# Order of products on TensorE in the feed-forward layers, and 64-blocks turned by a transpose on half of the partitions

## The chip, the core and the metric

The kernel runs on one core of a Trainium2 chip. It is written by hand for each engine: TensorE (PE, with its weight loads shown as PEld), VectorE (DVE), ScalarE (ACT), GpSimd (POOL), and SyncE (SP), which issues the DMAs. The metric is the device time of one execution in microseconds (us). Before the change the median of three runs is 1302.59 us (1301.69 to 1302.69).

## The reference

Everything is float32, with 256 tokens of 1024 channels. Three layers follow one another:

```
h = rwkv7_time_mix(x)                 # a recurrence over time, 16 heads of 64
x = layer_norm(ALPHA*x + h);  x = layer_norm(ALPHA*x + swiglu_ffn(x))      # ffn 0
h = moba_attention(x)                 # 16 heads of 64, causal
x = layer_norm(ALPHA*x + h);  x = layer_norm(ALPHA*x + swiglu_ffn(x))      # ffn 1
# second block: conv branch, sparse attention, cross attention, then
hf = rmsnorm(h) @ w_ff1;  h = h + square(relu(hf)) @ w_ff2                 # ffn 2
return rmsnorm(h)

def swiglu_ffn(x, w_in, w_down):      # w_in 1024 x 2*2816, w_down 2816 x 1024
    gate, up = split(x @ w_in, 2)
    return (silu(gate) * up) @ w_down
```

In ffn 2 the inner width is 4096 and there is one way in (`u`) instead of two (`g` and `u`).

## The kernel before

**Products in three parts.** A float32 operand of a large product is held as two fp32r tiles, high and low (`WH`, `WL` for weights, `AH`, `AL` or together `AHL` for activations, `HH`, `HL` for the inner activations of a feed-forward layer). `mm3` (L541 to L544) makes one product of three matmuls: high by high, high by low, low by high, all added up in one PSUM bank. A weight arrives as a piece of 1024 KB by DMA (`RG`); ACT rounds it to the high tile (L1506), DVE subtracts to get the low one (L2132). There are three such pairs of tiles, used in turn.

**The way in.** `wide_piece` computes 256 output channels for all 256 tokens from one piece, in two banks (m = 0, 1) and eight steps k of 128 input channels. A step (`wide_step`) is a pair of matmuls: a long one of 512 columns (L590; the high weight slice against `AH` and `AL` side by side, into the two halves of the bank) and a short one of 256 columns (L591; the low weight slice against `AH`, added to the second half). L590 and L591 run 864 times each, 54 pieces. The loops are m outside and k inside, but where the activations are just being made (`ready`: the first piece of ffn 0 and of ffn 1) k is outside. `wide_half` (L616, L618) does the same for 128 tokens at a time, with 256 and 128 columns, for two pieces. The last piece of each layer goes through `chan` (`mm3` with 256 columns).

**The way down.** `down(f, n, j, tt, ...)` adds the 256 inner channels of piece j to the output of 128 tokens (tt), for two output halves h of 512 channels in banks 4 + 2 tt + h. For each h and each of two slices m of inner channels, it runs `mm3`: stationary is a slice of `HH` or `HL`, moving are 512 columns of weights. That is 12 matmuls for a tt. The order is h outside, m inside. At the last j, the end of each h raises `s_dn` (for the last h of tt = 1, `s_wdone`). DVE waits for it in `ffn_parts` (L2274, then `ln_part` L2231 and L2234 for h = 0 and again for h = 1, `ln_scale`, and an L2132 for a later weight piece between the two tt) or, at the kernel's end, adds the sum to the residual (L2359).

**Turned blocks.** In the time mix, arrays hold two heads on partitions 0 to 63 and 64 to 127. `block_turn` (L929) and `turned` (L971) turn 64 x 64 blocks with an ordinary float32 matmul of the block against an identity; lower and upper partitions alternate. Together they turn 80 blocks on the lower partitions and 80 on the upper: 32 + 48 of each, over two halves of the heads. Elsewhere full 128 x 128 blocks are turned with `e.transpose` (L625, L673, L690, L755, L805, L1112).

The order of the work is the order of the code on each engine; semaphores tie the engines together. TensorE's program is one sequence. Of other engines only the lines that wait for it matter here.

Of the kernel before, what the change touches and what calls it, by code (L numbers as in the profile page):

```python
# [146 lines left out]
def build(nc, a, out):  # L147
    ctx = ExitStack()
    with ctx:
# [82 lines left out]
        ident = cst('ident')  # L232
# [169 lines left out]
        def half_k(k, tt):  # L402
            return slice(k * 256 + tt * 128, k * 256 + tt * 128 + 128)
# [136 lines left out]
        def mm3(e, o, l, r, start, stop):  # L540
            (lh, ll), (rh, rl) = l, r  # L541
            e.matmul(o, lh, rh, start=start, stop=False)  # L542
            e.matmul(o, lh, rl, start=False, stop=False)  # L543
            return e.matmul(o, ll, rh, start=False, stop=stop)  # L544
# [10 lines left out]
        def wsl(name, n, k, c0, c1):  # L555
            s = W[name] % NW
            return v3(WH[s], n)[:, k, c0:c1], v3(WL[s], n)[:, k, c0:c1]

        def tensor_program(e):
# [24 lines left out]
                        t = mm3(e, PS[b][:, m * 256:(m + 1) * 256], wsl(name, 256, k, m * 128, m * 128 + 128), act_k(k), k == 0, k == 7)  # L584
                t.then_inc(s_wdone, 1)

            def wide_step(name, b, m, k):

                wh, wl = wsl(name, 256, k, m * 128, m * 128 + 128)
                e.matmul(PS[b][:, :].rearrange("p (a t) -> p a t", a=2), wh, AHL[:, :, k * 256:k * 256 + 256], start=k == 0, stop=False)  # L590
                return e.matmul(PS[b][:, 256:512], wl, AH[:, k * 256:k * 256 + 256], start=False, stop=k == 7)  # L591

            def wide_piece(name, banks, ready=None):

                split_ready(name)
                if ready is None:
                    for m in range(2):
                        for k in range(8):
                            t = wide_step(name, banks[m], m, k)
                else:  # L600
                    for k in range(8):
                        if k % 2 == 0:
                            e.wait_ge(s_tl, ready + k // 2 + 1)
                        for m in range(2):
                            t = wide_step(name, banks[m], m, k)
                t.then_inc(s_wdone, 1)

            def wide_half(name, banks, tt, ready):

                if tt == 0:  # L610
                    split_ready(name)
                for k in range(8):
                    e.wait_ge(s_tl, ready + 8 * tt + k + 1)
                    for m, b in enumerate(banks):
                        wh, wl = wsl(name, 256, k, m * 128, m * 128 + 128)
                        e.matmul(PS[b][:, :].rearrange("p (a t) -> p a t", a=2)[:, :, tt * 128:tt * 128 + 128], wh, AHL[:, :, half_k(k, tt)],  # L616
                                 start=k == 0, stop=False)
                        t = e.matmul(PS[b][:, 256 + tt * 128:384 + tt * 128], wl, AH[:, half_k(k, tt)], start=False, stop=k == 7)  # L618
                if tt:
                    t.then_inc(s_wdone, 1)  # L620
# [96 lines left out]
            def down(f, n, j, tt, mem_units):  # L717

                if tt == 0:
                    split_ready(f'f{f}d{j}')  # L720
                    e.wait_ge(s_fhl, FFN_AT[f] + j + 1)
                    if j == 0:
                        e.wait_ge(s_mkvo, mem_units)
                for h in range(2):
                    for m in range(2):
                        c0 = m * 256 + tt * 128
                        hh = HH[:, j % 2, c0:c0 + 128], HL[:, j % 2, c0:c0 + 128]
                        t = mm3(e, PS[4 + 2 * tt + h][:, :], hh, wsl(f'f{f}d{j}', 1024, m, h * 512, h * 512 + 512),
                                j == 0 and m == 0, j == n - 1 and m == 1)
                    if (tt, h) == (1, 1):  # L730
                        t.then_inc(s_wdone, 1)
                    elif j == n - 1:
                        t.then_inc(s_dn, 1)

            def attention(A, i):
                at = A.at
# [187 lines left out]
            def block_turn(half, g, b):  # L924
                e.wait_ge(s_zb, 4 * half + g + 1)
                for n in range(4):
                    ns = slice(n * 64, n * 64 + 64)
                    for q in (slice(0, 64), slice(64, 128)):
                        t = e.matmul(PS[b][q, ns], Zq[q, g, ns], ident[q, q], start=True, stop=True)  # L929
                t.then_inc(s_zt, 1)  # L930

            decay(0)
# [31 lines left out]
            def turned(half, banks):  # L964

                for q in range(3):
                    for i, src in enumerate((BE, KA)):
                        b, o_ = (banks[i], 256 * q) if q < 2 else (banks[2], 256 * i)
                        for n in range(4):
                            for pp in E2:  # L970
                                t = e.matmul(PS[b][pp, o_ + 64 * n:o_ + 64 * n + 64], src[pp, 4 * half + n, 64 * q:64 * q + 64], ident[pp, pp],  # L971
                                             start=True, stop=True)
                        if q:
                            t.then_inc(s_tu, 1)

# [2032 lines left out]
```

## Time and profile before

| | |
|---|---|
| median of the runs | 1302.59 us |
| the profiled execution | 1302.25 us, its span 1300.4 us |
| PE busy | 1251.8 us, 96% |
| DVE busy, ACT busy | 901.3 us (69%), 641.2 us (49%) |
| L590 and L591 (way in), x864 each | 306.9 and 242.5 us busy |
| way down, x304 for each of L542, L543, L544 | 119.2, 118.6, 118.6 us busy |
| L929 and L971 (turned blocks), x128 and x192 | 4.1 and 6.0 us busy |

Busy times of matmuls overlap: a matmul is shown from its start to a modelled end, and the next one starts before that. What a matmul costs in a row of matmuls is the distance from its start to the next start, and the timeline gives that. A float32 product (not fp32r) stands in the trace as two records, which is why L971 has 192 records for 96 products. In the timeline a row with "x8" is eight equal instructions merged.

### The profile page before, as it was taken

Reading aid. Unit: us, or ns where it says so; the run is one execution under the profiler, and the core shown is the slowest. Engines: PE = TensorE matmul, PEld = TensorE weight load, DVE = VectorE, ACT = ScalarE, POOL = GpSimd, SP = SyncE. Lnnn points to the kernel's source line nnn. Section 1 sums busy time; section 2 is a strip of 40 time slices with the busy share of each in tenths; the row PEclk is TensorE's granted clock in tenths of the full one; section 3 lists DMA queues with packets and bytes.
Section 4 is the critical chain, followed back from the end, with each engine's and each line's share of the span. In section 5 each row is a group of like instructions: output and inputs, shape, how many; then the busy total and the mean of one; then the engine's idle time right before and its main releaser. Section 6 shows DMA issues by size and latency. Waiting matters only on the chain.

```text
span 1300.4 us, 22008 instructions
## 1 busy us (share of the span) xinstructions
PE 1251.8 (96%) x9332; PEld 1087.7 (84%) x9332; DVE 901.3 (69%) x1433; ACT 641.2 (49%) x966; POOL 69.7 (5%) x43
## 2 busy tenths in 40 slices
PE   6999998999999999999999998999999999999998
PEld 4788897888888988768888888999888987788886
DVE  7456766766655677656665567989999766665555
ACT  3433435464444455556444445444355556555553
POOL 0022000002000061000200010000000000000000
PEclk9999999999999999999999999999999999999999
DMA  9532201665555365326555537455544453355550
GB/s 306 171 109 88 75 4 58 204 227 194 195 195 181 110 229 180 114 94 226 195 194 184 186 117 241 134 162 169 163 150 158 141 162 104 123 201 191 192 179 33
DMA packets 156211, 205.97 MB, mean 158 GB/s; under 512 B 9904, under 2 KB 129840, under 8 KB 155984
## 3 DMA queue, kind: packets, MB, share of 16 engines
q1 hardware_dynamic: 156112, 204.55, 47.7%
q8 instruction: 74, 1.21, 0.4%
q14 instruction: 25, 0.20, 0.0%
HBM read 202.44 MB, written 1.05 MB: 156 GB/s over the span
## 4 chain that ended last, share of the span: by engine, by line
PE 72%; DVE 18%; ACT 7%; issue 2%; DMA 0%; DVEq 0%; SPq 0%; ACTq 0%
PE PS L590 15%; PE PS L542 11%; PE PS L544 11%; PE PS L543 11%; PE PS L591 8%; DVE WW L2132 5%; PE PS L949 4%; DVE PH L2717 4%; ACT WW L1506 2%; DVE PA L2371 1%; PE PS L880 1%; PE PS L920 1%; PE PS L1004 1%; ACT Xb L1535 1%; PE PS L656 1%
## 5 line engine op out<-in xcount | busy, mean ns | idle before, releaser
L2132 DVE TENSOR_TENSOR WW<-RG,WW 128x2048 fp32r<-128x2048 f32 x164 | 380.9, 2337 | 142.2 <-ACT WW L1506 142.0
L1506 ACT ACTIVATE WW<-RG 128x2048 fp32r<-128x2048 f32 x164 | 311.2, 1906 | 30.6 <-PE PS L544 25.4
L590 PE MATMUL PS<-AHL,WW 128*128 128x512 f32 x864 | 306.9, 399 | 0.5 <-DVE WW L2132 0.5
L591 PE MATMUL PS<-AHL,WW 128*128 128x256 f32 x864 | 242.5, 281 | 0.0
L542 PE MATMUL PS<-AHL,WW 128*128 128x256 f32 x704 | 203.4, 289 | 2.5 <-DVE AHL L2171 1.8
L543 PE MATMUL PS<-AHL,WW 128*128 128x256 f32 x704 | 199.2, 283 | 0.0
L544 PE MATMUL PS<-AHL,WW 128*128 128x256 f32 x704 | 199.2, 283 | 0.0
L590 PEld LDWEIGHTS PS<-AHL,WW 128*128 128x128 f32 x864 | 162.3, 188 | 41.0 <-DVE WW L2132 1.2
L591 PEld LDWEIGHTS PS<-AHL,WW 128*128 128x128 f32 x864 | 163.2, 189 | 1.2
L542 PEld LDWEIGHTS PS<-AHL,WW 128*128 128x128 f32 x704 | 134.9, 192 | 5.3 <-issue 3.7
L543 PEld LDWEIGHTS PS<-AHL,WW 128*128 128x128 f32 x704 | 135.0, 192 | 1.7 <-issue 1.4
L544 PEld LDWEIGHTS PS<-AHL,WW 128*128 128x128 f32 x704 | 134.9, 192 | 0.0
L542 PE MATMUL PS<-WW,HH 128*128 128x512 f32 x304 | 119.2, 392 | 0.4 <-issue 0.2
L543 PE MATMUL PS<-WW,HH 128*128 128x512 f32 x304 | 118.6, 390 | 0.0
L544 PE MATMUL PS<-WW,HL 128*128 128x512 f32 x304 | 118.6, 390 | 0.0
L1608 ACT ACTIVATE PF<-PS 128x256 f32<-128x256 f32 x110 | 36.2, 381 | 135.5 <-PE PS L591 135.3
L2717 DVE SCALAR_TENSOR_TENSOR PH<-PH,VB 128x256 f32<-128x256 f32 x240 | 97.8, 478 | 0.0
L2282 DVE TENSOR_TENSOR PF<-PF,PS 128x256 f32<-128x256 f32 x110 | 41.3, 417 | 51.9 <-ACT PF L1608 50.3
L542 PEld LDWEIGHTS PS<-WW,HH 128*128 128x128 f32 x304 | 57.1, 188 | 13.4 <-issue 1.1
L544 PEld LDWEIGHTS PS<-WW,HL 128*128 128x128 f32 x304 | 57.1, 188 | 12.6
L543 PEld LDWEIGHTS PS<-WW,HH 128*128 128x128 f32 x304 | 57.1, 188 | 10.8
L949 PE MATMUL PS<-PA,RG 128*128 128x256 f32 x256 | 58.4, 383 | 0.0
(369 smaller groups left out, 1848.3 us busy)
## 6 DMA issues: line engine op xcount, KB each, us to landing
RG<-in_ffn_w_in SPq DMA_DIRECT2D x44, 1024.0 KB, 5.2
RG<-in_w_ff SPq DMA_DIRECT2D x32, 1024.0 KB, 5.4
RG<-in_w_in SPq DMA_DIRECT2D x30, 1024.0 KB, 5.2
RG<-in_ffn_w_down SPq DMA_DIRECT2D x22, 1024.0 KB, 4.9
RG<-in_w_rkv SPq DMA_DIRECT2D x12, 1024.0 KB, 6.8
RG<-in_moba_w_qkv SPq DMA_DIRECT2D x12, 1024.0 KB, 7.4
RG<-in_w_o SPq DMA_DIRECT2D x4, 1024.0 KB, 7.7
RG<-in_wx_kv SPq DMA_DIRECT2D x4, 1024.0 KB, 5.6
```

Of the source, the lines that this page charges most:

```text
L542: e.matmul(o, lh, rh, start=start, stop=False)
L543: e.matmul(o, lh, rl, start=False, stop=False)
L544: return e.matmul(o, ll, rh, start=False, stop=stop)
L590: e.matmul(PS[b][:, :].rearrange("p (a t) -> p a t", a=2), wh, AHL[:, :, k * 256:k * 256 + 256], start=k == 0, stop=False)
L591: return e.matmul(PS[b][:, 256:512], wl, AH[:, k * 256:k * 256 + 256], start=False, stop=k == 7)
L656: t = e.matmul(MEM_AT[u], wv[:, k, u % 2 * 128:u % 2 * 128 + 128], MT[:, k, :], start=k == 0, stop=k == 7)
L949: t = e.matmul(PS[n][:, m * 256:m * 256 + 256], v3(ring(name), 256)[:, k, m * 128:m * 128 + 128], XM[slot][:, k, :], start=k == 0, stop=k ...
L1506: s.activation(WH[hi_n % NW], ring(SPLIT[hi_n]), ACT.Copy, bias=0.0, scale=1.0).then_inc(s_hi, 1)
L1608: t = s.activation(dst[:, 256 * m:256 * m + 256], PS[b][:, 256:512], ACT.Copy, bias=0.0, scale=1.0)
L2132: v.tensor_tensor(WL[lo_n % NW], ring(SPLIT[lo_n]), WH[lo_n % NW].bitcast(F32), ALU.subtract).then_inc(s_lo, 1)
L2282: t = v.tensor_tensor(dst[:, sl], dst[:, sl], PS[b][:, 0:256], ALU.add)
L2717: v.scalar_tensor_tensor(out=CV[:, k, :], in0=UB[:, k, i:i + 256], scalar=vec(f'cw{i}', k), in1=CV[:, k, :], op0=ALU.mult, op1=ALU.add).th ...
```

## The change

Three edits, all in TensorE's program. In the way in, eight long matmuls of a bank come first and then its eight short ones (with `ready`, four long and four short; in `wide_half` two long and two short). In the way down, both output halves take the products of one slice of `HH` (four matmuls), then of `HL` (two), before the next slice; both halves now end at the last two matmuls. In the turned blocks, the lower partitions use `e.transpose`, the upper ones keep the matmul.

```diff
-            def wide_step(name, b, m, k):
+            def wide_hi(name, b, m, k):
-                wh, wl = wsl(name, 256, k, m * 128, m * 128 + 128)
+                wh, _ = wsl(name, 256, k, m * 128, m * 128 + 128)
                 e.matmul(PS[b][:, :].rearrange("p (a t) -> p a t", a=2), wh, AHL[:, :, k * 256:k * 256 + 256], start=k == 0, stop=False)
+            def wide_lo(name, b, m, k):
+                _, wl = wsl(name, 256, k, m * 128, m * 128 + 128)
                 return e.matmul(PS[b][:, 256:512], wl, AH[:, k * 256:k * 256 + 256], start=False, stop=k == 7)
...
                     for m in range(2):
                         for k in range(8):
-                            t = wide_step(name, banks[m], m, k)
+                            wide_hi(name, banks[m], m, k)
+                        for k in range(8):
+                            t = wide_lo(name, banks[m], m, k)
                 else:
-                    for k in range(8):
-                        if k % 2 == 0:
-                            e.wait_ge(s_tl, ready + k // 2 + 1)
+                    for kp in range(4):
+                        e.wait_ge(s_tl, ready + kp + 1)
                         for m in range(2):
-                            t = wide_step(name, banks[m], m, k)
+                            for k in (2 * kp, 2 * kp + 1):
+                                wide_hi(name, banks[m], m, k)
+                        for m in range(2):
+                            for k in (2 * kp, 2 * kp + 1):
+                                t = wide_lo(name, banks[m], m, k)
...
-                for h in range(2):
-                    for m in range(2):
-                        c0 = m * 256 + tt * 128
-                        hh = HH[:, j % 2, c0:c0 + 128], HL[:, j % 2, c0:c0 + 128]
-                        t = mm3(e, PS[4 + 2 * tt + h][:, :], hh, wsl(f'f{f}d{j}', 1024, m, h * 512, h * 512 + 512),
-                                j == 0 and m == 0, j == n - 1 and m == 1)
-                    if (tt, h) == (1, 1):
-                        t.then_inc(s_wdone, 1)
-                    elif j == n - 1:
-                        t.then_inc(s_dn, 1)
+                o_ = [PS[4 + 2 * tt + h][:, :] for h in range(2)]
+                for m in range(2):
+                    c0 = m * 256 + tt * 128
+                    hh, hl = HH[:, j % 2, c0:c0 + 128], HL[:, j % 2, c0:c0 + 128]
+                    w = [wsl(f'f{f}d{j}', 1024, m, h * 512, h * 512 + 512) for h in range(2)]
+                    first, last = j == 0 and m == 0, j == n - 1 and m == 1
+                    for h in range(2):
+                        e.matmul(o_[h], hh, w[h][0], start=first, stop=False)
+                        e.matmul(o_[h], hh, w[h][1], start=False, stop=False)
+                    for h in range(2):
+                        t = e.matmul(o_[h], hl, w[h][0], start=False, stop=last)
+                        if last and (tt, h) != (1, 1):
+                            t.then_inc(s_dn, 1)
+                if tt:
+                    t.then_inc(s_wdone, 1)
...
-                    for q in (slice(0, 64), slice(64, 128)):
-                        t = e.matmul(PS[b][q, ns], Zq[q, g, ns], ident[q, q], start=True, stop=True)
+                    for q in E2:
+                        if q.start:
+                            t = e.matmul(PS[b][q, ns], Zq[q, g, ns], ident[q, q], start=True, stop=True)
+                        else:
+                            t = e.transpose(PS[b][q, ns], Zq[q, g, ns], ident[q, q])
```

`turned` gets the same edit as `block_turn`, and `wide_half` the same as the way in. No other engine's sequence changes.

On PE in ffn 0, the last steps of a way-in piece before (`PS3` is a bank, `WW` the weight tiles, `AHL` the activations):

```order
L590 MATMUL PS3<-AHL,WW 128x512
L591 MATMUL PS3<-AHL,WW 128x256
L590 MATMUL PS3<-AHL,WW 128x512
L591 MATMUL PS3<-AHL,WW 128x256
L590 MATMUL PS3<-AHL,WW 128x512
L591 MATMUL PS3<-AHL,WW 128x256
```

The same piece now, whole (L595 is the short matmul):

```order
L590 MATMUL PS2<-AHL,WW 128x512 [waits w_lo,ffn_summed]
L590 MATMUL PS2<-AHL,WW 128x512 x7
L595 MATMUL PS2<-AHL,WW 128x256 x8
L590 MATMUL PS3<-AHL,WW 128x512 x8
L595 MATMUL PS3<-AHL,WW 128x256 x8
```

Long and short no longer alternate: a bank takes eight of 512 columns, then eight of 256.

On PE, the first way down that follows, tokens tt = 0, before (`HH`, `HL` the inner activations; `PS4` is output half 0, `PS5` half 1):

```order
L542 MATMUL PS4<-WW,HH 128x512 [waits mem_out,ffn_lo,w_lo]
L543 MATMUL PS4<-WW,HH 128x512
L544 MATMUL PS4<-WW,HL 128x512
L542 MATMUL PS4<-WW,HH 128x512
L543 MATMUL PS4<-WW,HH 128x512
L544 MATMUL PS4<-WW,HL 128x512
L542 MATMUL PS5<-WW,HH 128x512
L543 MATMUL PS5<-WW,HH 128x512
L544 MATMUL PS5<-WW,HL 128x512
L542 MATMUL PS5<-WW,HH 128x512
L543 MATMUL PS5<-WW,HH 128x512
L544 MATMUL PS5<-WW,HL 128x512
```

The same twelve now (L742 and L743 take `HH`, L745 takes `HL`):

```order
L742 MATMUL PS4<-WW,HH 128x512 [waits mem_out,ffn_lo,w_lo]
L743 MATMUL PS4<-WW,HH 128x512
L742 MATMUL PS5<-WW,HH 128x512
L743 MATMUL PS5<-WW,HH 128x512
L745 MATMUL PS4<-WW,HL 128x512
L745 MATMUL PS5<-WW,HL 128x512
L742 MATMUL PS4<-WW,HH 128x512
L743 MATMUL PS4<-WW,HH 128x512
L742 MATMUL PS5<-WW,HH 128x512
L743 MATMUL PS5<-WW,HH 128x512
L745 MATMUL PS4<-WW,HL 128x512
L745 MATMUL PS5<-WW,HL 128x512
```

The count is the same. Half 0 (`PS4`) had its last matmul in the sixth place, and now has it in the eleventh; half 1 stays at the twelfth.

## Rows read from the trace of the kernel before

**Rows 1.** The page: busy time by engine, and granted TensorE clock by slice.
```profile
PE 1251.8 (96%) x9332; PEld 1087.7 (84%) x9332; DVE 901.3 (69%) x1433; ACT 641.2 (49%) x966; POOL 69.7 (5%) x43
...
PEclk9999999999999999999999999999999999999999
```
**Rows 2.** Waits of PE, longest in total: us, times, longest.
```profile
PE PS L820 <- DVE PA L2371: 7.5, 2, 7.2
```
**Rows 3.** Timeline of PE in ffn 1, way in: start, duration, instruction.
```profile
600.17 0.28 PE L591 MATMUL PS<-AHL,WW 128*128 128x256 f32 x1
600.29 0.40 PE L590 MATMUL PS<-AHL,WW 128*128 128x512 f32 x1
...
604.41 0.28 PE L591 MATMUL PS<-AHL,WW 128*128 128x256 f32 x1
```
**Rows 4.** Timeline of PE, 512 columns after a run of 256.
```profile
435.29 0.40 PE L542 MATMUL PS<-WW,HH 128*128 128x512 f32 x1
...
437.13 0.39 PE L544 MATMUL PS<-WW,HL 128*128 128x512 f32 x1
```
**Rows 5.** Timeline of PE, 256 columns after a run of 512.
```profile
423.77 0.28 PE L542 MATMUL PS<-AHL,WW 128*128 128x256 f32 x1
...
425.08 0.28 PE L544 MATMUL PS<-AHL,WW 128*128 128x256 f32 x1
```
**Rows 6.** Timeline of PE, two pairs of `wide_half` shown.
```profile
1110.72 0.34 PE L616 MATMUL PS<-AHL,WW 128*128 128x256 f32 x1
...
1112.58 0.33 PE L616 MATMUL PS<-AHL,WW 128*128 128x256 f32 x1
```
**Rows 7.** Timeline of PE, end of ffn 1.
```profile
765.39 0.39 PE L544 MATMUL PS<-WW,HL 128*128 128x512 f32 x1
...
766.52 0.39 PE L543 MATMUL PS<-WW,HH 128*128 128x512 f32 x1
```
**Rows 8.** Timeline of DVE after ffn 1, and PE's next wait, in brackets.
```profile
765.88 0.69 DVE L2231 SCALAR_TENSOR_TENSOR Sb<-Hb,PS 128x512 f32<-128x512 f32 x1 [2.03 <-PE PS L544]
...
769.59 2.29 DVE L2132 TENSOR_TENSOR WW<-RG,WW 128x2048 fp32r<-128x2048 f32 x1
771.79 0.68 DVE L2231 SCALAR_TENSOR_TENSOR Sb<-Hb,PS 128x512 f32<-128x512 f32 x1
...
780.94 1.09 PE L690 MATMUL PS<-CB,Sb 128*128 128x128 f32 x8 [1.46 <-DVE Sb L2205]
```
**Rows 9.** Timeline of ACT and PE after ffn 0.
```profile
449.38 0.81 ACT L1600 ACTIVATE Sb<-Sb,ST 128x512 f32<-128x512 f32 x1 [0.42 <-DVE ST L2244]
450.52 1.04 PE L690 MATMUL PS<-CB,Sb 128*128 128x128 f32 x8
```
**Rows 10.** Timeline of PE and DVE at the kernel's end.
```profile
1292.35 0.39 PE L544 MATMUL PS<-WW,HL 128*128 128x512 f32 x1
1292.77 0.69 DVE L2359 TENSOR_TENSOR Hb<-Hb,PS 128x512 f32<-128x512 f32 x1 [0.30 <-PE PS L544]
...
1293.70 0.39 PE L544 MATMUL PS<-WW,HL 128*128 128x512 f32 x1
...
1294.13 0.69 DVE L2359 TENSOR_TENSOR Hb<-Hb,PS 128x512 f32<-128x512 f32 x1 [0.67 <-PE PS L544]
```
**Rows 11.** Timeline of PE: turned blocks of the first half, and full transposes.
```profile
144.63 2.99 PE L971 MATMUL PS<-CB,PA 64*64 64x64 f32 x96
...
446.20 1.03 PE L690 MATMUL PS<-CB,Sb 128*128 128x128 f32 x8
```
**Rows 12.** Waits of ACT, 130 to 200 us: us, times, longest.
```profile
ACT KX L1762 <- PE PS L971: 15.2, 2, 8.9
```
**Rows 13.** Timeline of PE: from a full array to 64 rows of it.
```profile
488.38 0.28 PE L544 MATMUL PS<-AHL,WW 128*128 128x256 f32 x1
488.59 0.93 PE L782 MATMUL PS<-PH 64*128 64x128 f32 x8
```

More of the change, by code:

```diff
@@ L614, in wide_half @@
                     for m, b in enumerate(banks):
-                        wh, wl = wsl(name, 256, k, m * 128, m * 128 + 128)
+                        wh, _ = wsl(name, 256, k, m * 128, m * 128 + 128)
                         e.matmul(PS[b][:, :].rearrange("p (a t) -> p a t", a=2)[:, :, tt * 128:tt * 128 + 128], wh, AHL[:, :, half_k(k, tt)],
                                  start=k == 0, stop=False)
+                    for m, b in enumerate(banks):
+                        _, wl = wsl(name, 256, k, m * 128, m * 128 + 128)
                         t = e.matmul(PS[b][:, 256 + tt * 128:384 + tt * 128], wl, AH[:, half_k(k, tt)], start=False, stop=k == 7)
@@ L970, in turned @@
                             for pp in E2:
-                                t = e.matmul(PS[b][pp, o_ + 64 * n:o_ + 64 * n + 64], src[pp, 4 * half + n, 64 * q:64 * q + 64], ident[pp, pp],
-                                             start=True, stop=True)
+                                to, of = PS[b][pp, o_ + 64 * n:o_ + 64 * n + 64], src[pp, 4 * half + n, 64 * q:64 * q + 64]
+                                if pp.start:
+                                    t = e.matmul(to, of, ident[pp, pp], start=True, stop=True)
+                                else:
+                                    t = e.transpose(to, of, ident[pp, pp])
                         if q:
```

## The prediction, made before the changed kernel was run

> **What bounds the kernel now.** I read the page first: PE is busy for 96% of the span, the granted clock is at nine tenths or more of full in every slice (the 2.4 GHz level), and DVE, the next, has 69% [rows 1]. Then the waits of PE: the longest in total is 7.5 us, and it lies in the first stage [rows 2]. So in the feed-forward layers the time is the number of matmuls times their distance in a row, and other engines matter only where a layer ends. The distances come from the timeline, start to start, since the busy times of matmuls overlap.
>
> **The way in, 104 blocks.** Today long and short alternate. Twelve pairs take from 600.17 to 604.41, so a pair is 4.24 / 12 = 0.3533 us and eight pairs are 2.827 [rows 3]. No place of the trace has eight long ones and then eight short ones of this kind, but both changes of length occur between longer runs. After a run of 256 columns the first eight distances at 512 columns go from 435.29 to 437.13, 1.84 us, that is 0.230 each [rows 4]. Once settled they are closer: the five from 765.39 to 766.52 give 1.13 / 5 = 0.226 [rows 7]. After a run of 512 columns the first eleven distances at 256 columns take from 423.77 to 425.08, 1.31 us, so eight take 0.95 [rows 5]. A block of eight and eight then is 1.84 + 0.95 = 2.79, against 2.827: 0.037 less. What costs today is thus the change of length itself, not the length. 52 pieces have two such blocks each (54, less the two that use `ready`): 104 x 0.037 = 3.8 us. In the 30 pieces that follow a way down, the first eight long ones find PE settled at 0.226 to 0.227 and take 1.81 instead of 1.84: 30 x 0.03 = 0.9. Today's first pair there gains little from this, and I take off 0.3. Sum: **4.4 us less**. All of it lies on PE's own row with nothing beside it that would end later, since PE hardly waits for weights here.
>
> The bounds. If a long one against `AHL` costs what it costs today because it reads two stretches of memory, and not because of its neighbours, nothing is won: 0. At best each pair falls to 0.2265 + 0.12 = 0.3465 at once: 832 x 0.0068 = 5.7 us less. I take 4.4, since the evidence of rows 4 and 5 is on plain matmuls of the same lengths and type.
>
> **`ready` and `wide_half`.** With `ready` the blocks are four and four; the next piece then waits for its low weights, so nothing counts: 0. In `wide_half` eight pairs of 256 and 128 columns take from 1110.72 to 1112.58, 0.2325 a pair or 0.116 a matmul [rows 6], although 128 columns are half the work of 256. So each matmul, however short, seems to wait for its own weight load, and two long and two short ones have four loads as before: 0. If the short ones did cost half of 0.12 when side by side, two pairs would fall from 0.465 to 0.36, and 32 such groups would give 3.4 us; that is the bound below, and 0.3 us more is the bound above (32 x 0.01, if all four come to 0.12).
>
> The Trainium skill ("TensorE: Matmul & The Clock Gate", LDWEIGHTS) has a load take its columns divided by 1.2 GHz, whatever the product's length, which is an estimate of 107 ns for 128 columns; the 116 ns of rows 6 fit that, and the rule speaks for no gain in `wide_half`.
>
> **The way down, inside.** 912 matmuls before, 912 now, all of 512 columns, each with its own load. Neighbours of one length settle at 0.226 to 0.227 whichever bank or slice they use [rows 7], so the sharing of a slice is worth 0; nothing in the trace shows a second use of a slice to be cheaper. Bounds: a hundredth of a slot either way, 0.002 us, which is what these rows leave open by their rounding, 2 us in all.
>
> **The way down, at its end.** Here the change costs. Half 0 now ends with the eleventh matmul instead of the sixth, five slots later: from 765.39 to 766.52, 1.13 us [rows 7].
> - *ffn 1.* DVE starts on half 0 of tt = 0 at 765.88, 0.49 after the start of that matmul, having idled 2.03 us for it. From there it works without a gap worth naming: both halves, the scale, the low weights at 769.59 for 2.29 us, and at 771.79 half 0 of tt = 1, when its matmuls have been done for a while. So the later start of tt = 0 moves the whole chain by 1.13, and PE, which waits 1.46 us for the end of it already, waits 1.13 more [rows 8].
> - *ffn 0.* The same chain and the same 1.13. It ends with L1600, 449.38 + 0.81 = 450.19, and PE takes its transposes at 450.52 without having waited, so 0.33 us of cover less some 0.06 for the signal: 1.13 - 0.27 = 0.86 [rows 9].
> - *The end of the kernel.* Half 0 of tt = 1 is added at 1292.77, 0.42 after its L544 at 1292.35; half 1 at 1294.13, 0.43 after 1293.70. Now half 0 ends one slot before half 1, at 1293.47, so its add runs from 1293.90 for 0.69 us and half 1's starts at about 1294.62: 0.49 us later, and the norm, the scale and the output behind it too [rows 10]. Half 0 of tt = 0 also comes later, but has 3 us of slack.
>
> Sum: 1.13 + 0.86 + 0.49 = **2.5 us more**. Bounds: 1.6 (if ffn 0 had full cover) and 3.4 (three times 1.13).
>
> **The turned blocks.** 96 records of L971, two for each of 24 blocks below and 24 above, take 2.99 us from 144.63: 0.03 a record, and 0.12 for a lower and an upper block together, since records of different partitions run beside each other and records of the same ones follow at 0.06. A transpose stands in the trace with one record (eight for the eight of L690 [rows 11]), so a lower block has one instead of two. The upper block keeps its two, 0.12 in a row, and sets the pace: 0. Bounds below: if records went one by one at 0.03, 80 x 0.03 = 2.4 us less. Bounds above: if the transpose can't run beside the upper block's records, 80 x 0.06 = 4.8 us more; if PE has to be switched between transpose and product, as it does between a full array and 64 rows of it, where 0.21 us lie between two starts instead of the 0.12 of rows 5 [rows 13], it is 160 x 0.09 = 14.4 us more. ACT waits for `turned` [rows 12], so neither gain nor loss would be hidden for the first half of the heads. I take 0, as all turned blocks keep 64 x 64 tiles and no switch is in the code.
>
> The Trainium skill speaks against this edit: "TensorEngine Tiling (Array Packing)", Restrictions and Gotchas, has column tiling exclude the transpose mode for FP32 and FP32R input, and Key Properties has a change of tiling mode drain TensorE. By that, either the transposes run as ordinary products (0) or each is a switch, which is the 14.4 us case. The trace has no transpose on a 64 x 64 tile, so only the price of a switch is borne out, by rows 13.
>
> **Sum.** -4.4 + 2.5 + 0 = -1.9 us. The profiled execution took 1302.25 us, 1.85 more than its span, and 0.34 less than the median 1302.59; so 1300.35 for it, and 1300.7 us for the median.
>
> **Rivals.**
> - *A, the forecast*, 1300.7 us: chance 0.48. Its spread is 1299.3 to 1302.3 (way in between 3.2 and 5.7, ends between 1.6 and 3.4).
> - *B, alternation was not the cost*: the two stretches of `AHL` are, so way in 0, ends +2.5: 1305.1 us. For it: today's 0.3533 is only seen with `AHL` in two stretches. Against: rows 4 shows plain matmuls at 0.230 for a while after a change of length. Chance 0.13.
> - *C, cheaper than that*: the way in at its best (5.7) with `wide_half` or the turned blocks giving 2 us or more, or the ends hidden: about 1298 us. Against: PE's wait of 1.46 in rows 8, and rows 6. Chance 0.20.
> - *D, the transposes hurt*: from the point on at which a lower transpose can't share the array with the upper product. 1300.7 + 4.8 = 1305.5, or with a switch each way 1315.1. For it: no 64 x 64 transpose has been seen, and the upper partitions were left as they are. Against: nothing in the code changes the tile. Chance 0.12 and 0.07.
>
> 0.2%, 2.6 us, is about what can be told from no change. Faster by more (below 1300.0): C and a quarter of A, 0.32. Slower by more (above 1305.2): D and some of B, 0.22. Within: 0.46. The range takes in A, B, most of C and the cheaper D: 1298.0 to 1305.5 us, and leaves out the switch.
>
> **What would show it.** Way in: distances near 0.230 after the first long one, falling, and 0.12 for the short ones, eight and eight in 2.79. Wrong if the long ones stay at 0.236. Ends: PE's wait before the second L690 group after ffn 1 grows to 2.6 us, one of about 0.9 appears after ffn 0, and the second add at the end starts 0.9 to 1.0 us after the last matmul instead of 0.43. Turned blocks: the 48 blocks of `turned` for one half of the heads in 2.9 us again; 4.4 or more would be D. The forecast as a whole is wrong if the way in saves less than 3 us, or if the DVE chain at a layer's end turns out to start at another signal than half 0's.

## The result, and the profile after

The changed kernel takes 1339.28 us (median of 4 runs, 1337.85 to 1339.44), the kernel before 1302.14 us beside it (1300.98 to 1302.69). The ratio is 1.0284, 95% interval 1.0266 to 1.0302: slower by 37 us, where 1.9 us less was forecast, and above the forecast's range, which ended at 1305.5 us.

The page shows the same picture as before in its first line and another one in its last, and that is the first thing to read here (busy time by engine; granted clock by slice of 33.4 us):

```profile
PE 1289.1 (96%) x9252; PEld 1114.9 (83%) x9252; DVE 900.6 (67%) x1433; ACT 641.4 (48%) x966; POOL 69.8 (5%) x43
...
PEclk9999796999999999999999999999999999999999
```

PE has 80 records fewer and is busy for 37.3 us more; DVE and ACT do the same work in the same time. The clock, at 9 (90% or more) in every slice before [rows 1], is at 7 and 6 in the fifth and seventh slice. Both are in the time mix, where the turned blocks are. Stretch by stretch (busy time and count of each engine, granted clock, DMA share, GB/s):

```profile
130.00:140.00 10.00, 10.00 (x57) 5.07 (x57) 7.96 (x15) 2.56 (x5) 1.27 (x1) 0.94 0.71 249
140.00:150.00 10.00, 10.00 (x122) 8.84 (x123) 4.26 (x8) 0.77 (x2) 0.00 (x0) 0.72 0.01 2
...
160.00:170.00 10.00, 10.00 (x114) 7.88 (x116) 1.72 (x5) 3.69 (x11) 0.00 (x0) 0.52 0.00 0
...
210.00:220.00 10.00, 10.00 (x50) 6.38 (x48) 2.56 (x4) 1.65 (x4) 0.00 (x0) 0.53 0.01 2
220.00:230.00 10.00, 10.00 (x59) 6.56 (x59) 0.00 (x0) 1.57 (x5) 0.00 (x0) 0.50 0.00 1
```

For comparison a stretch of the kernel before with `turned` in it:

```profile
140.00:150.00 10.00, 9.85 (x271) 9.67 (x269) 6.86 (x13) 3.42 (x10) 0.00 (x0) 1.00 0.01 2
```

From 210 to 230 us PE is busy all the time by the profile, starts 109 records in 20 us (271 stood in the 10 us above, before), and runs at half of full clock (0.50 to 0.53, the 1.2 GHz level). DVE and ACT nearly stand still. The timeline of PE shows what it does (start, duration, instruction). L948 is the transpose of a lower block and L946 the product of an upper one, two records:

```profile
135.02 0.24 PE L948 MATMUL PS<-CB,Sb 64*64 64x64 f32 x1
135.19 0.33 PE L946 MATMUL PS<-CB,Sb 64*64 64x64 f32 x2
135.45 0.24 PE L948 MATMUL PS<-CB,Sb 64*64 64x64 f32 x1
...
141.44 0.31 PE L948 MATMUL PS<-CB,Sb 64*64 64x64 f32 x1
141.68 0.47 PE L946 MATMUL PS<-CB,Sb 64*64 64x64 f32 x2
142.08 0.31 PE L948 MATMUL PS<-CB,Sb 64*64 64x64 f32 x1
...
142.97 0.47 PE L896 MATMUL PS<-PA 64*64 64x128 f32 x1
```

A lower and an upper block together take 0.43 us at full clock (135.02 to 135.45), and 0.64 at half clock (141.44 to 142.08). Before they took 0.12 [rows 11]. Of the 0.43, 0.17 lie between the transpose and the product, and 0.26 from the product's first record to the next transpose. The 128 records of L896 that follow are slower too: from 142.97 to the start of L883 at 151.30 are 8.33 us, where the same work took 6.99 us before (136.74 to 143.73).

`turned` has the same pattern. The timeline further on, where L883 begins, `turned` begins (L994) and ends (L1011) in the first half of the heads, and where it and the `block_turn` behind it begin and end in the second:

```profile
151.30 1.14 PE L883 MATMUL PS<-CB,PA 64*64 64x2 f32 x32
152.38 0.24 PE L994 MATMUL PS<-CB,PA 64*64 64x64 f32 x1
...
165.62 0.36 PE L1011 MATMUL PS<-Sb,PA 64*64 64x64 f32 x1
...
206.19 0.24 PE L994 MATMUL PS<-CB,PA 64*64 64x64 f32 x1
...
219.44 0.31 PE L948 MATMUL PS<-CB,Sb 64*64 64x64 f32 x1
...
229.28 0.36 PE L1011 MATMUL PS<-Sb,PA 64*64 64x64 f32 x1
```

Each group of turned blocks is counted from its first start to the first start of what follows it. The four groups take 7.95 (135.02 to 142.97), 13.24, 13.25 and 9.84 us, 44.3 together. Before they took 1.92, 2.83, 2.80 and 1.87, 9.4 together: 34.9 us more. ACT pays in waiting. Over both halves of the heads (130 to 240 us) it waits 25.0 and 9.0 us for `turned`, where before, in the same two places, it waited 15.2 [rows 12] and 0.6:

```profile
ACT KX L1784 <- PE PS L992: 25.0, 2, 14.6
...
ACT KX L1787 <- PE PS L992: 9.0, 2, 4.5
```

The other two edits did what was forecast. In ffn 1, long (L590) and short (L595) matmuls in rows of eight:

```profile
636.64 2.00 PE L590 MATMUL PS<-AHL,WW 128*128 128x512 f32 x8
638.48 1.11 PE L595 MATMUL PS<-AHL,WW 128*128 128x256 f32 x8
639.43 1.78 PE L590 MATMUL PS<-AHL,WW 128*128 128x512 f32 x7
```

Eight and eight take 639.43 - 636.64 = 2.79 us, against 2.83 in [rows 3]. PE's waits for the two lines that make the input of its full transposes, at the ends of ffn 0 and ffn 1 among others (us in total, times, longest; before 2.0 in two for the first, and 1.8 in two, the longest 1.5, for the second):

```profile
PE PS L701 <- ACT Sb L1622: 2.7, 3, 1.0
PE PS L701 <- DVE Sb L2227: 2.6, 1, 2.6
```

The end of the kernel, PE's last two matmuls and DVE's last two adds, each pair in one row:

```profile
1330.37 0.61 PE L745 MATMUL PS<-WW,HL 128*128 128x512 f32 x2
```

```profile
1330.80 1.28 DVE L2381 TENSOR_TENSOR Hb<-Hb,PS 128x512 f32<-128x512 f32 x2 [1.05 <-PE PS L745]
```

The second add ends at 1332.08 and takes 0.69 [rows 10], so it starts at 1331.39, 0.79 after the last matmul at 1330.60.

### The profile page after: what moved, and what is told of

Same layout as the page of the kernel before. It is cut to its first block, busy times and chain, and to the rows that moved or that the text cites. A ratio compares the mean times of both kernels' runs of the same rounds, so it can differ in the third digit from the quotient of the medians.

```text
span 1337.6 us, 21848 instructions
## 1 busy us (share of the span) xinstructions
PE 1289.1 (96%) x9252; PEld 1114.9 (83%) x9252; DVE 900.6 (67%) x1433; ACT 641.4 (48%) x966; POOL 69.8 (5%) x43
## 4 chain that ended last, share of the span: by engine, by line
PE 73%; DVE 18%; ACT 7%; issue 2%; DMA 0%; DVEq 0%; SPq 0%; ACTq 0%
PE PS L590 14%; PE PS L595 7%; PE PS L542 6%; PE PS L544 6%; PE PS L543 6%; DVE WW L2154 5%; PE PS L742 5%; PE PS L743 5%; PE PS L745 5%; PE PS L968 4%; DVE PH L2739 4%; ACT WW L1528 2%; PE PS L992 1%; PE PS L896 1%; DVE PA L2393 1%
## 5 line engine op out<-in xcount | busy, mean ns | idle before, releaser
L590 PE MATMUL PS<-AHL,WW 128*128 128x512 f32 x864 | 216.9, 392 | 0.5 <-DVE WW L2154 0.5
L542 PE MATMUL PS<-AHL,WW 128*128 128x256 f32 x704 | 203.3, 289 | 2.1 <-DVE AHL L2193 1.3
L543 PE MATMUL PS<-AHL,WW 128*128 128x256 f32 x704 | 199.1, 283 | 0.0
L544 PE MATMUL PS<-AHL,WW 128*128 128x256 f32 x704 | 199.1, 283 | 0.0
L590 PEld LDWEIGHTS PS<-AHL,WW 128*128 128x128 f32 x864 | 157.0, 189 | 30.0 <-DVE WW L2154 0.9
L542 PEld LDWEIGHTS PS<-AHL,WW 128*128 128x128 f32 x704 | 134.9, 192 | 4.9 <-issue 3.3
L543 PEld LDWEIGHTS PS<-AHL,WW 128*128 128x128 f32 x704 | 135.0, 192 | 1.7 <-issue 1.4
L544 PEld LDWEIGHTS PS<-AHL,WW 128*128 128x128 f32 x704 | 134.9, 192 | 0.0
L595 PEld LDWEIGHTS PS<-AHL,WW 128*128 128x128 f32 x864 | 118.4, 190 | 8.8
L595 PE MATMUL PS<-AHL,WW 128*128 128x256 f32 x864 | 121.1, 282 | 0.0
L742 PE MATMUL PS<-WW,HH 128*128 128x512 f32 x304 | 118.7, 390 | 0.5 <-issue 0.3
L743 PE MATMUL PS<-WW,HH 128*128 128x512 f32 x304 | 118.8, 391 | 0.0
L745 PE MATMUL PS<-WW,HL 128*128 128x512 f32 x304 | 93.7, 389 | 0.0
L745 PEld LDWEIGHTS PS<-WW,HL 128*128 128x128 f32 x304 | 57.1, 188 | 12.1
L742 PEld LDWEIGHTS PS<-WW,HH 128*128 128x128 f32 x304 | 57.2, 188 | 11.8 <-issue 1.1
L743 PEld LDWEIGHTS PS<-WW,HH 128*128 128x128 f32 x304 | 57.2, 188 | 10.8
```

What stands on the lines that cost most here:

```text
L742: e.matmul(o_[h], hh, w[h][0], start=first, stop=False)
L743: e.matmul(o_[h], hh, w[h][1], start=False, stop=False)
L745: t = e.matmul(o_[h], hl, w[h][0], start=False, stop=last)
```

## The experiments

Ten kernels, each timed beside the kernel before on the same chip. Two theories on the transposes: **S**, that each change between a transpose and a product on TensorE empties it; **P**, that a 64 x 64 transpose is itself slow. A third question was whether the lower clock is a cause or a result.

| run | median us | before | ratio, 95% interval |
|---|---|---|---|
| e1_no_turn | 1300.44 | 1302.39 | 0.9982 [0.9973, 0.9991] |
| e2_turn_only | 1341.52 | 1302.39 | 1.0300 [1.0286, 1.0314] |
| e3_wide_only | 1298.51 | 1302.39 | 0.9970 [0.9959, 0.9981] |
| e4_down_only | 1304.81 | 1302.39 | 1.0022 [1.0012, 1.0032] |
| e5_group_control | 1302.78 | 1302.0 | 1.0006 [0.9997, 1.0015] |
| e6_turn_grouped | 1319.13 | 1302.0 | 1.0131 [1.0117, 1.0145] |
| e7_turn_far | 1309.86 | 1302.0 | 1.0058 [1.0043, 1.0073] |
| e8_early_end | 1297.7 | 1302.0 | 0.9966 [0.9954, 0.9979] |
| e9_wide16 | 1296.53 | 1302.2 | 0.9956 [0.9943, 0.9970] |
| e10_turn_first | 1309.61 | 1302.2 | 1.0058 [1.0045, 1.0072] |

### e1_no_turn: the change without the transposes

```diff
-                        if q.start:
-                            t = e.matmul(PS[b][q, ns], Zq[q, g, ns], ident[q, q], start=True, stop=True)
-                        else:
-                            t = e.transpose(PS[b][q, ns], Zq[q, g, ns], ident[q, q])
+                        t = e.matmul(PS[b][q, ns], Zq[q, g, ns], ident[q, q], start=True, stop=True)
```
The same in `turned`.

> The change without its transposes (way in and way down as changed, the turned blocks as before). Theory S (the transposes on 64 x 64 tiles cost nearly all of the 37 us, by lost overlap and by the clock that falls with it; the two other edits are worth what the prediction said): 1.9 us less than before, between 0.5 and 3.5 less; no half-clock stretch in the time mix. Rival R (the long-first order or the shared slice costs too, for example through the clock after the longer wait behind ffn 1): more than before by 3 us or more.

1.95 us faster than before: -1.9 was the forecast of the two edits it keeps. The changed kernel is 37.1 us slower than before, so 39.1 us of it go with the transposes.

### e2_turn_only: the kernel before with the transposes alone

The edit of e1, the other way round, on the kernel before.

> The kernel before with the transposes alone. Theory S: 1302 + 37 + 2 = 1341 us, within 2; a lower and an upper block together 0.43 us at the full clock and 0.64 at half, in place of 0.12, and the same half-clock stretches in the time mix. Rival R: under 1335, since a part of the loss belongs to the other edits.

39.1 us slower. The transposes are enough by themselves, and it is what e1 leaves for them: nothing hangs on the edits together.

### e3_wide_only: the way in alone

The first two hunks of the change, and `wide_half`.

> The kernel before with only the way in and wide_half reordered. The prediction's term: 4.4 us less (3.2 to 5.7). Rival W (the gain on the long and short matmuls of a row is given back at the ends of the pieces, where other engines set the time): under 1.5 us less. Eight long and eight short should take 2.79 us.

3.9 us faster, where 4.4 was the term. Summed over all 864 pairs, the distances from start to start fall from 306.5 us in the kernel before to 302.8, which is 3.7. In `wide_half` a group of four takes 460 ns against 464 before: 0, as forecast. Behind a way down the timeline of PE has the first eight long ones faster:

```profile
614.93 1.98 PE L590 MATMUL PS<-AHL,WW 128*128 128x512 f32 x8
616.74 1.11 PE L595 MATMUL PS<-AHL,WW 128*128 128x256 f32 x8
617.70 2.00 PE L590 MATMUL PS<-AHL,WW 128*128 128x512 f32 x8
619.54 1.12 PE L595 MATMUL PS<-AHL,WW 128*128 128x256 f32 x8
```

1.81 us for the eight at 614.93, and 1.84 for the next. A whole block behind a way down takes 2.77 us, but the first eight pairs behind a way down were faster before as well, 2.81 instead of 2.83. So each of the 104 blocks gains the same 0.037, 3.8 us in all, and the 0.6 that the forecast added for the 30 pieces behind a way down is not there.

### e4_down_only: the way down alone

The hunk of `down`.

> The kernel before with only the way down changed. The prediction's term: 2.5 us more (1.6 to 3.4), all at the ends of the three layers: 0.9 after ffn 0, 1.1 after ffn 1, 0.5 at the kernel's end. Rival C (the longer wait after ffn 1 also drops the granted clock, as one short half-clock stretch stands there in the changed kernel's trace and none in the one before): 3.5 us more or above, with a half-clock stretch behind that wait. Rival N (other work covers it): under 1 us more.

2.4 us slower, where 2.5 was the term. Its timeline of DVE after ffn 1, the first step on half 0 (idle before it in brackets):

```profile
768.49 0.69 DVE L2236 SCALAR_TENSOR_TENSOR Sb<-Hb,PS 128x512 f32<-128x512 f32 x1 [3.16 <-PE PS L734]
```

The timeline of PE there, the two groups of transposes:

```profile
783.53 1.09 PE L690 MATMUL PS<-CB,Sb 128*128 128x128 f32 x8 [2.58 <-DVE Sb L2210]
785.01 1.97 PE L690 MATMUL PS<-CB,Sb 128*128 128x128 f32 x8 [0.39 <-DVE Sb L2210]
```

DVE idles 3.16 us instead of 2.03, and PE 2.58 instead of 1.46 [rows 8]: 1.13 and 1.12 more, one for one, and what the forecast said. The second group takes 1.97 us, where it took 1.09 before. The granted clock is 0.66 over these 10 us, and was 1.00 there before:

```profile
783.00:793.00 10.00, 7.95 (x45) 7.35 (x46) 6.46 (x14) 7.06 (x15) 0.00 (x0) 0.66 0.91 296
```

### e5_group_control: four lower blocks, then four upper, all as products

```diff
-                for n in range(4):
...
-                    for q in (slice(0, 64), slice(64, 128)):
+                for q in E2:
+                    for n in range(4):
...
```
The same in `turned`.

> The kernel before, turned blocks all by matmul, but in each group of four first the four lower blocks and then the four upper ones, 20 groups. It says what the order alone costs. Four lower blocks then have eight records one after the other at 0.058 with nothing beside them: 0.93 us a group in place of 0.47, 9 us more in all, if lower and upper no longer run beside each other. If TensorE looks far enough ahead to pair them anyway: 0 to 2 us.

No difference (0.8 us, the interval holds 1). The 9 us that I expected of grouping are not there: the records of one kind of block follow at 0.06 us, and upper records start between lower ones, those of one group's upper four beside the lower four of the next. Only the first four of a group stand alone. So this is a clean control for e6.

### e6_turn_grouped: e5 with the lower four as transposes

```diff
+                        if q.start:
+                            t = e.matmul(PS[b][q, ns], Zq[q, g, ns], ident[q, q], start=True, stop=True)
+                        else:
+                            t = e.transpose(PS[b][q, ns], Zq[q, g, ns], ident[q, q])
```
The same in `turned`.

> As the group control, with the lower four of each group as transposes. Theory S (the price is at each change between transpose and product, some 0.16 us for each at the full clock, since the pipeline empties): 40 changes in place of 160; a group takes 4 x 0.06 + 8 x 0.058 + 2 changes at 0.1 to 0.16, about 0.95 us, so within 3 us of the group control, with no or short half-clock stretches. Rival P (each transpose on a 64 x 64 tile is slow by itself, whatever stands beside it): transposes still 0.15 us or more apart in a row, 4 to 8 us above the group control. Rival L (a transpose only fails to run beside a product on other partitions): equal to or below the group control.

16.4 us over its control, between 39 with 160 changes and 0 with none. Neither theory had this size (S said within 3, P 4 to 8). Its timeline of PE:

```profile
135.74 0.41 PE L932 MATMUL PS<-CB,Sb 64*64 64x64 f32 x4
136.08 0.67 PE L930 MATMUL PS<-CB,Sb 64*64 64x64 f32 x8
136.69 0.41 PE L932 MATMUL PS<-CB,Sb 64*64 64x64 f32 x4
```

A group takes 0.95 us: 0.34 for four transposes up to the first product, 0.61 for eight records and the way back. In e5 four pairs need 4 x 0.12 = 0.48, so 0.47 more for two changes and for the lost sharing: 20 groups, 9.4 us. Four transposes at 0.056 and eight records at 0.058 make 0.69, so the two changes are 0.26 of the 0.95, 0.13 each. The alternating pair has the same price: 0.43 less 0.17 for its three records. The rest goes with the clock: the 20 groups take 23.1 us in all, 4 more than 20 x 0.95, and the other products at half clock are slower too. It is at half in the second half of the heads, where it was at 1.00 before:

```profile
200.00:210.00 10.00, 10.00 (x89) 8.38 (x90) 2.01 (x4) 2.81 (x8) 0.00 (x0) 0.50 0.01 3
```

### e7_turn_far: in `turned`, 24 transposes in a row and then 24 products

```diff
+                for pp in E2:
+                    for q in range(3):
+                        for i, src in enumerate((BE, KA)):
...
```
`block_turn` as in e6: 20 changes in all.

> As the grouped one, but turned has all its 24 transposes first and then the 24 upper products; 4 changes there in place of 24, 20 in the kernel. Theory S: a further 20 changes less, 2 to 3 us below the grouped one. Rival P: the same as the grouped one within 1 us. The distance from transpose to transpose is read in the row of 24: S expects 0.06 or less, P 0.15.

7.9 us slower than before, and 9.3 faster than e6, where S had said 2 to 3 and P less than 1. Half the clock is a part of that too: in e7 the clock falls only at the first `block_turn`, in e6 at all four groups. Its timeline of PE in `turned` (L978 transposes, L976 products):

```profile
149.49 1.53 PE L978 MATMUL PS<-CB,PA 64*64 64x64 f32 x24
150.94 1.26 PE L976 MATMUL PS<-CB,PA 64*64 64x64 f32 x18
```

24 transposes start and are followed by the first product within 1.45 us, 0.06 each, and 0.056 inside the row. That is no slower than a product's record. P is refuted: what costs is the change between the two, and what is lost besides is that a lower and an upper block no longer run at once (24 x 0.06 = 1.4 us for each half; `turned` takes 4.1 and 4.4 us instead of 2.8).

### e10_turn_first: only the first 16 of the lower blocks, alternating

```diff
-                    for q in (slice(0, 64), slice(64, 128)):
-                        t = e.matmul(PS[b][q, ns], Zq[q, g, ns], ident[q, q], start=True, stop=True)
+                    for q in E2:
+                        if q.start or half:
+                            t = e.matmul(PS[b][q, ns], Zq[q, g, ns], ident[q, q], start=True, stop=True)
+                        else:
+                            t = e.transpose(PS[b][q, ns], Zq[q, g, ns], ident[q, q])
```

> Only the first block_turn (16 lower blocks of 80) by transposes, alternating as in the change. The empty pipeline alone: 16 x 0.31 = 5.0 us more. With the clock: the changed kernel took 8.1 us there instead of 1.9, and 1.0 us more for the products behind it at half clock, so 7 us more, 6 to 8. If the stretch of half clock goes on for longer than in the changed kernel or is gone, the clock follows something else than these transposes.

7.4 us slower, inside what was expected. The timeline gives the parts:

```profile
134.70 0.24 PE L932 MATMUL PS<-CB,Sb 64*64 64x64 f32 x1
...
142.66 8.73 PE L880 MATMUL PS<-PA 64*64 64x128 f32 x127
...
151.13 1.09 PE L867 MATMUL PS<-CB,PA 64*64 64x2 f32 x31
```

Up to the second record of L880, `block_turn` takes 7.96 us instead of 1.92: 6.0 more, of which 16 x 0.31 = 5.0 is the change of kind at full clock, and 1.0 that the last pairs ran at half clock. L880's 128 records behind it take 8.5 instead of 7.0, since the lower clock lasts into them. By stretches:

```profile
140.00:150.00 10.00, 10.00 (x121) 9.06 (x123) 4.43 (x8) 0.77 (x2) 0.00 (x0) 0.70 0.01 2
150.00:160.00 10.00, 9.86 (x315) 9.75 (x313) 6.45 (x14) 4.18 (x12) 0.00 (x0) 1.00 0.01 3
```

Here the clock falls during the alternation and returns after it, and from 150 to 220 us, where the changed kernel has it at half again, it stays at 1.00. In the time mix the half clock is a result of the alternating transposes, and then a cost of its own to whatever comes next.

### e8_early_end: way in and shared slice, but the last j in the old order

```diff
+                if j == n - 1:
+                    for h in range(2):
+                        for m in range(2):
+                            c0 = m * 256 + tt * 128
+                            hh = HH[:, j % 2, c0:c0 + 128], HL[:, j % 2, c0:c0 + 128]
+                            t = mm3(e, PS[4 + 2 * tt + h][:, :], hh, wsl(f'f{f}d{j}', 1024, m, h * 512, h * 512 + 512), False, m == 1)
+                        t.then_inc(s_wdone if (tt, h) == (1, 1) else s_dn, 1)
+                    return
```
No transposes.

> Way in as changed and way down with the shared slice, but at the last j of each layer the old order, in which half 0 ends six matmuls ahead; turned blocks as before. Expected: the gain of the way in alone, 3.9 us less than before (within 0.7), PE's wait after ffn 1 back at 1.5 us and no half-clock stretch there. If the shared slice itself has a cost or a gain inside the layers, it shows as the difference to the way-in-only kernel.

4.3 us faster than before, 2.4 better than e1, to which it is the same but for the last j. Its waits at the ends of the layers are those of before:

```profile
PE PS L701 <- ACT Sb L1624: 2.0, 2, 1.0
PE PS L701 <- DVE Sb L2229: 1.8, 2, 1.5
```

So the whole cost of the way down sits in which half ends early at the last j, and the shared slice at all other j is worth nothing that can be told (e8 against e3: -4.3 and -3.9). The clock surprised me: it falls here as well, behind the old wait of 1.5 us.

```profile
775.00:785.00 10.00, 7.79 (x42) 7.19 (x43) 6.71 (x14) 7.30 (x15) 0.00 (x0) 0.66 0.99 316
```

The dip seen in e4 does not need the longer wait. It does not need the way down either: within 10 us of this place the clock also falls in the changed kernel, in e1, in e2 (transposes alone, 0.66 from 820 to 830) and in e9 (way in alone, 0.83 from 775 to 785), and not in e3, e5, e6, e7 and e10. The kernel before has such a dip too, elsewhere, behind a wait of PE for 2.8 us:

```profile
220.00:230.00 10.00, 6.59 (x83) 5.54 (x84) 7.54 (x14) 5.25 (x10) 0.00 (x0) 0.90 0.80 267
```

Every kernel but e8 has one behind that wait. In the traces one such dip moves what follows by 0.4 us (e9, after ffn 1) to 1.6 us (the one above, which e8 does not have), so a difference of that size between two single executions is not to be read as the work of an edit.

### e9_wide16: the way in alone, 16 long ones of both banks and then 16 short

```diff
                         for k in range(8):
-                            t = wide_step(name, banks[m], m, k)
+                            wide_hi(name, banks[m], m, k)
+                    for m in range(2):
+                        for k in range(8):
+                            t = wide_lo(name, banks[m], m, k)
```

> Only the way in changed, with both banks' sixteen long matmuls first and then their sixteen short ones: half as many changes of length as with eight and eight. If a change of length costs what the eight-long rows show (1.84 us where settled ones take 1.81, less 0.007 on the first short one), 52 changes less are worth 52 x 0.02 = 1.0 us on top of the 3.9 of the way-in-only kernel: 4.9 us less than before (4.2 to 5.6). If the gain came from something else in the order, such as fewer switches of the stationary tile in a bank: no more than 3.9.

5.7 us faster than before, just above the expected 4.2 to 5.6, the best of all, and a version that beats both kernels. Its way in, in ffn 1:

```profile
600.22 2.08 PE L595 MATMUL PS<-AHL,WW 128*128 128x256 f32 x16
602.13 3.82 PE L590 MATMUL PS<-AHL,WW 128*128 128x512 f32 x16
605.79 0.40 PE L595 MATMUL PS<-AHL,WW 128*128 128x256 f32 x2
```

16 and 16 take 5.57 us (600.22 to 605.79), against 2 x 2.79 in rows of eight. Over all 864 pairs the distances sum to 301.8 us, 1.0 less than in e3, as expected. The medians differ by 2.0, from different chips and with overlapping intervals, so only the 1.0 of the traces can be put down to the longer rows.

## Why the prediction was wrong, step by step

- **What bounds the kernel.** Right as far as it went: the time did change on PE's own row. But "the granted clock is at full, so count distances" took the clock for given. In the time mix it fell with what PE was given to do, and a change to PE's mix of instructions has to be asked what it does to the clock.
- **Way in, -4.4.** Right but for 0.6: -3.9 by e3, 3.7 of it in the distances, and nothing extra behind a way down. Eight and eight at 2.79, the first eight after a way down at 1.81, both as worked out from rows 4 and 5. Alternation was the cost, not the two stretches of `AHL`; rival B falls.
- **`wide_half`, 0.** Right, 460 against 464 ns for four.
- **Way down inside, 0.** Right within what can be told (e8 against e3).
- **Ends of the layers, +2.5.** Right: 2.4 by e4, and the parts in the traces add up to 2.2 to 2.4. ffn 1 was 1.12 for 1.13, ffn 0 0.7 to 0.9 by the waits for 0.86. At the kernel's end, DVE's second add starts 0.79 us after the last matmul instead of 0.43: 0.36 for 0.49, since the two adds follow each other at 0.59 and not at the 0.72 that I assumed.
- **Turned blocks, 0: this step failed**, by 39 us. The prediction said: "The upper block keeps its two, 0.12 in a row, and sets the pace: 0", because "all turned blocks keep 64 x 64 tiles and no switch is in the code". But the upper block does not go on beside a transpose: next to one, a pair takes 0.43 instead of 0.12. The bound above had the right count (160 changes) and the wrong price. 0.09 a change came from rows 13, where only the number of rows changes; here a change there and back is 0.31 at full clock, lost sharing included. 80 x 0.31 = 24.8 us; the half clock, under which 53 of the 80 pairs fall, adds what is left of the 34.9, 10 us; and 3.6 us more lie in the products between and behind the turned blocks: L1026, behind the last group, starts at 234.74, and the same instruction before (L1004) at 196.02, 38.7 later; 0.2 of it is there when the first group begins (135.02 against 134.82), and the groups account for 34.9 of the 38.5.
- **The sum.** -3.9 + 2.4 = -1.5, and e1 has -1.95. With 39.1 for the transposes (e2), that is +37.

The price is not one of every change between a transpose and a product. The kernel before has such changes on full 128 x 128 tiles. Eight transposes [rows 11], sixteen records of a product, eight transposes [rows 9] and the product again follow each other in its timeline like this:

```profile
447.07 3.62 PE L656 MATMUL PS<-PA,RG 128*128 128x256 f32 x16
...
451.40 0.81 PE L656 MATMUL PS<-PA,RG 128*128 128x256 f32 x3
```

The eight transposes take 0.87 us up to the product (446.20 to 447.07) and 0.88 the second time, 0.11 each, which is also their distance in a row. The sixteen records take 3.45 us (447.07 to 450.52), 0.216 each, also their distance in a row. So a change costs nothing there, in either direction. Where such a group stands between products on 64 x 64 tiles, eight full transposes take 1.02 us instead of 0.87:

```profile
195.00 1.09 PE L673 MATMUL PS<-CB,PA 128*128 128x128 f32 x8
196.02 0.68 PE L1004 MATMUL PS<-Sb,Xb 64*64 64x64 f32 x16
```

There the tile changes on either side. With the 0.15 from the last 64 x 64 product before to the first transpose (194.85 to 195.00), where 0.06 is usual, the two changes of tile cost 0.24 us. The two changes in e6 cost 0.26. So a 64 x 64 transpose next to a 64 x 64 product costs what a change of tile does, though the code names the same tile size. That it is one is an inference from the sizes, not shown.

The two rules of the Trainium skill ("TensorEngine Tiling (Array Packing)") that stood beside this step come out so. That column tiling excludes the transpose mode for FP32 does not keep such a transpose from running here: on the lower partitions they ran, at 0.056 us each in a row. Whether TensorE ran them with column tiling no run shows. That a change of tiling mode drains TensorE agrees in kind with the 0.24 above, and its size stands on no page. If a 64 x 64 transpose is itself outside the tiling mode, the two rules together give what was measured; that was not tested. I had weighed the rule by the price of another change. A rule that speaks against an edit should have got the chance of its mechanism (0.07 for the switch) from how well the counter-evidence held, and that was only "nothing in the code changes the tile".

**What stays open.** Why a 64 x 64 transpose and a product hold each other up is not shown, only that they do, on this tile, and what it costs; "empties" in theory S is a picture of it. Inside the groups of all these runs the transposes were on the lower partitions and the products on the upper ones, so a change of kind on the same partitions of a 64 x 64 tile was not tried either. Neither is it shown what makes the clock fall: in e2, e6, e7 and e10 it falls 2 to 5 us after the first changes of kind, with PE at 100% busy by the profile, but the short dips behind a wait of PE come without any transposes in the turned blocks, in the kernel before too. Whether the upper blocks as transposes too (no change of kind at all) would beat the products was not tried.

## What to carry to other kernels

An instruction that saves a pass (a transpose instead of a float32 product) is priced with its neighbours and on its tile: on 64 x 64, alternating with products, it cost 0.31 us each time and half the clock; in a row it took no longer than one record of a product; on full tiles the change cost nothing. Put instructions of one kind and one length together, and count the changes (on 64 x 64 here 160 of kind for +39 us, 40 for +17, 20 for +8 against the kernel before, with the lost sharing and the lower clock in it, so not in proportion; for lengths 0.04 us a block). Where something else waits for one of two outputs, keep the order in which it ends early for the last pass only: that took back all of the way down's 2.4 us. And where an operation has no neighbour in the trace like those it will have, the range has to hold the bound of that mechanism times its count, and the bound should not come from another kind of change.

## What the runs showed of the hardware

- On a 64 x 64 tile, transposes of float32 follow each other at 56 ns (e7), the same as one record of a product (58 ns). A transpose next to a product: 0.17 us until the product, 0.15 back, where 0.06 is usual.
- On full 128 x 128 tiles a change between transposes and products costs nothing: 0.11 us from the last transpose to the product, 0.216 back, both as in a row (before).
- The granted clock fell to 0.5 with PE busy at 100% in the profile. The count of records in a stretch (109 in 20 us, where 271 stood in 10) shows how little such a row starts, the busy share doesn't.
- At half clock a pair of transpose and product took 0.64 instead of 0.43 us.
- Lower and upper blocks, all as products, run beside each other even if four of each come in a row (e5).
- After a change of length, matmuls of 512 columns start at 0.23 us apart and settle at 0.227 over about eight.
